# Pool products of a hybrid decoder layer: three float32r passes from split operands, two attention units later, in place of native fp32

## The reference, cut to what matters

```python
h    = rms_norm(x, norm_mix_pre)
proj = h @ w_in                                   # (1024, 1792), split by columns
u_pool, g_b, g_c, u_conv, q, k, v = split(proj)   # 256, 256, 256, 256, 512, 128, 128
# pool mixer: per group g of 64 channels a causal trailing mean over 2, 4, 8, 16
# tokens, minus the token; then a 64x64 map of the group, and a scale per channel
d = mean_w(u_pool) - u_pool
y_pool = einsum('bsgc,gcd->bsgd', d, pool_w) * pool_scale
mix = concat(y_pool, y_conv, y_attn) @ w_o
x   = x + rms_norm(mix, norm_mix_post)            # then a gated conv-MLP, untouched here
```

## Time and profile before

| | |
|---|---|
| median of three runs | 950.24 us (950.16 to 950.44) |
| span of the profiled execution | 948.2 us, so 2.0 us less than the median |
| TensorE matmul, busy | 938.9 us, 99% |
| TensorE weight load, busy | 777.9 us, 82% |
| VectorE, busy | 654.7 us, 69% |
| ScalarE, busy | 433.5 us, 46% |
| GpSimd, busy | 189.4 us, 20% |
| DMA | 151.16 MB, mean 159 GB/s |

### The profile page before, as it was taken

The page is one execution under the profiler, slowest core; times in us unless marked ns, Lnnn a source line. Parts: engine busy times, 40 slices in busy tenths (PEclk is TensorE's granted clock), DMA queues, the critical chain, the costliest instruction groups (busy, mean ns, idle before and its releaser), DMA issues.

```text
span 948.2 us, 11487 instructions
## 1 busy us (share of the span) xinstructions
PE 938.9 (99%) x4419; PEld 777.9 (82%) x4419; DVE 654.7 (69%) x710; ACT 433.5 (46%) x648; POOL 189.4 (20%) x182
## 2 busy tenths in 40 slices
PE   8999999999999999999999999999999999999997
PEld 7988887887888888888888888888888888888886
DVE  6645795766655899777877787778776653535668
ACT  5524444444433555445443444444444454335353
POOL 3301000000111424242223333443431100000021
PEclk9999999999999999999999999999999999999999
DMA  6999971005322236486343446554647775677455
GB/s 225 269 328 231 209 145 45 23 23 178 134 89 89 90 97 206 142 184 183 115 141 100 145 112 133 112 143 105 140 91 208 201 235 214 228 267 264 163 171 200
DMA packets 114248, 151.16 MB, mean 159 GB/s; under 512 B 6289, under 2 KB 66193, under 8 KB 114193
## 3 DMA queue, kind: packets, MB, share of 16 engines
q1 hardware_dynamic: 100737, 118.63, 38.5%
q0 software_dynamic: 13456, 31.79, 16.8%
HBM read 113.17 MB, written 60.29 MB: 183 GB/s over the span
## 4 chain that ended last, share of the span: by engine, by line
PE 97%; DVE 1%; DMA 0%; ACT 0%; POOL 0%; issue 0%; DVEq 0%; POOLq 0%; SPq 0%; ACTq 0%
PE ps L1616 30%; PE ps L1618 30%; PE ps L1617 30%; PE ps L1626 1%; PE ps L1751 1%; PE ps L1774 1%; PE ps L1752 1%; PE ps L1760 1%; PE ps L1778 1%; DMA xin<-in_x 0%; DVE hlo L1138 0%; PE ps L1789 0%; DVE ps L1155 0%; PE ps L1664 0%; DVE x2b L1427 0%
## 5 line engine op out<-in xcount | busy, mean ns | idle before, releaser
L1616 PE MATMUL ps<-hhi,whi 128*128 128x512 f32 (+1 forms) x240 | 91.1, 379 | 0.5 <-DVE hlo L1138 0.5
L1618 PE MATMUL ps<-hhi,wlo 128*128 128x512 f32 (+1 forms) x240 | 88.5, 369 | 0.0
L1617 PE MATMUL ps<-hlo,whi 128*128 128x512 f32 (+1 forms) x240 | 88.5, 369 | 0.0
L686 POOL TENSOR_TENSOR w_sums<-wraw 128x1024 f32<-128x1024 f32 x20 | 48.4, 2421 | 185.8 <-DVE w2lo L1373 63.0
L648 POOL TENSOR_SCALAR meansq<-sumsq 128x1 f32<-128x1 f32 x28 | 10.0, 357 | 373.4 <-ACT yg L1042 170.8
L1616 PEld LDWEIGHTS ps<-hhi,whi 128*128 128x128 f32 x240 | 45.3, 189 | 8.0 <-DVE hlo L1138 0.7
L1001 ACT ACTIVATE yg<-ps,par_b 128x1024 f32<-128x1024 f32 x21 | 25.3, 1207 | 57.9 <-DVE ps L1499 57.9
L1618 PEld LDWEIGHTS ps<-hhi,wlo 128*128 128x128 f32 x240 | 45.2, 189 | 7.7
L1617 PEld LDWEIGHTS ps<-hlo,whi 128*128 128x128 f32 x240 | 45.3, 189 | 7.4 <-issue 0.5
L1447 DVE SCALAR_TENSOR_TENSOR yg<-ps,par_a,yg 128x1023 f32<-128x1023 f32 x22 | 28.2, 1282 | 26.9 <-ACT yg L1001 26.9
L1616 PE MATMUL ps<-h2hi,whi 128*128 128x512 f32 x116 | 45.4, 391 | 0.2 <-DVE wraw L1148 0.2
(11 more groups left out here) (261 smaller groups left out, 2709.1 us busy)
## 6 DMA issues: line engine op xcount, KB each, us to landing
wraw<-in_ffn_w_up SPq DMA_DIRECT2D x42, 512.0 KB, 5.2
s_dram<-in_ffn_w_down POOLq DMA_DIRECT2D x6, 2816.0 KB, 28.1
wraw<-r_dram SPq DMA_DIRECT2D x44, 256.0 KB, 3.7
wraw<-s_dram SPq DMA_DIRECT2D x44, 256.0 KB, 4.9
r_dram<-cst SPq DMA_DIRECT2D x33, 256.0 KB, 2.8
wraw<-act_dram SPq DMA_DIRECT2D x33, 256.0 KB, 3.6
wraw<-in_ffn_w_down SPq DMA_DIRECT2D x33, 256.0 KB, 4.6
wraw<-in_w_in SPq DMA_DIRECT2D x14, 512.0 KB, 10.2
```

The source lines that it names most:

```text
L686: pool.tensor_tensor(w_sums[:, 0:2, :], raw[:, 0:4:3, :], raw[:, 2:3, :].broadcast_to([P, 2, HALF]), ALU.add)\
L1616: pe.matmul(acc, w_hi, x_hi, start=first, stop=False, skip_group_check=looped)
L1617: pe.matmul(acc, w_hi, x_lo, start=False, stop=False, skip_group_check=looped)
L1618: return pe.matmul(acc, w_lo, x_hi, start=False, stop=last, skip_group_check=looped)
```

## The change

The pool products go from slots 8 and 10 to slots 10 and 12. Each is made of three float32r passes in place of one native fp32 matmul, through the helper `product`. For that both operands are split. ScalarE rounds `pool_mat` after the exponentials of unit 6, the first half of `pool_d` after the evacuation in unit 8, and the second half in unit 10, behind the copy of the first product, into the same tile `pool_hi`. VectorE makes the low parts in `mixer_work`: that of the matrix (128x256) in unit 7 ahead of the longer sums, that of the first half (128x1024) in unit 9, and that of the second in unit 11 ahead of the conv taps. The copies of the products follow their slots, to units 10 and 12. The new tiles lie over space that is free at that time.

```diff
-POOL_SLOT = (8, 10)
+POOL_SLOT = (10, 12)
...
+            def round_pool_mat():
+                act.wait_ge(pool_w_in, 64)
+                act.activation(pool_mat_hi[:, :, :], pool_mat[:, :, :], ACT.Copy)\
+                   .then_inc(pool_mat_rounded, 1)
+
+            def round_pool(i):
+                if i == 0:
+                    act.wait_ge(pool_ready, 2)
+                else:
+                    act.wait_ge(pool_mixed, 1)
+                act.activation(pool_hi[:, :], pool_d[:, i, :], ACT.Copy).then_inc(pool_rounded, 1)
...
                 exps(u)
                 if u in POOL_SLOT:
                     copy_pooled(POOL_SLOT.index(u))
+                if u == 6:
+                    round_pool_mat()
                 if u == 8:
                     evacuate(2)
+                    round_pool(0)
+                if u == POOL_SLOT[0]:
+                    round_pool(1)
...
+            def low_pool_mat():
+                dve.wait_ge(pool_mat_rounded, 1)
+                dve.tensor_tensor(pool_mat_lo[:, :, :], pool_mat[:, :, :], pool_mat_hi[:, :, :],
+                                  ALU.subtract).then_inc(pool_mat_split, 1)
+
+            def low_pool(i):
+                dve.wait_ge(pool_rounded, i + 1)
+                dve.tensor_tensor(pool_lo[:, i, :], pool_d[:, i, :], pool_hi[:, :], ALU.subtract)\
+                   .then_inc(pool_split, 1)
...
             def mixer_work(u):
 
                 s = u // 2 - 2
+                if u == 7:
+                    low_pool_mat()
                 if u == 8:
                     pool_means(1)
+                if u == 9:
+                    low_pool(0)
+                if u == 11:
+                    low_pool(1)
...
             def pool_product(i):
-                if i == 0:
-                    pe.wait_ge(pool_w_in, 64)
-                pe.wait_ge(pool_ready, i + 1)
+                pe.wait_ge(pool_mat_split, 1)
+                pe.wait_ge(pool_split, i + 1)
                 pe.wait_ge(s_masked, POOL_SLOT[i] + 1)
                 for c in range(2):
-                    last = pe.matmul(ps[:, 4 + c, :], pool_mat[:, i, :],
-                                     pool_d[:, i, c * HALF:(c + 1) * HALF],
-                                     start=True, stop=True)
+                    cols = slice(c * HALF, (c + 1) * HALF)
+                    last = product(ps[:, 4 + c, :], pool_mat_hi[:, i, :], pool_mat_lo[:, i, :],
+                                   pool_hi[:, cols], pool_lo[:, i, cols], True, True)
                 last.then_inc(pool_mixed, 1)
```

More of the change, by code:

```diff
@@ L174, in build @@
         par_rows = alloc(xb_, "par_rows", [P, 2, P])
+        pool_mat_hi = alloc(xb_, "pool_mat_hi", [P, 2, P], F32R)
         xb_.close()
@@ L180, in build @@
         xb2.close()
+        xb3 = ExitStack()
+        alloc(xb3, "under_pool_hi", [P, 3 * SEQ])
+        pool_hi = alloc(xb3, "pool_hi", [P, SEQ], F32R)
+        alloc(xb3, "under_pool_lo", [P, 2 * SEQ + 3 * PAD])
+        pool_lo = alloc(xb3, "pool_lo", [P, 2, SEQ], F32R)
+        alloc(xb3, "under_pool_mat_lo", [P, NT, P])
+        pool_mat_lo = alloc(xb3, "pool_mat_lo", [P, 2, P], F32R)
+        xb3.close()
         xc = ExitStack()
@@ L319, in build @@
         pool_ready = sem("pool_d_ready")
+        pool_mat_rounded = sem("pool_weights_rounded")
+        pool_mat_split = sem("pool_weights_split")
+        pool_rounded = sem("pool_d_rounded")
+        pool_split = sem("pool_d_split")
         pool_mixed = sem("pool_product_done")
```

## The result

The changed kernel takes **953.44 us** (median of five, 952.30 to 954.87), the kernel before on the same chip 950.24 (950.16 to 950.59). The ratio is 1.0032, with a 95% interval of 1.0021 to 1.0042: slower, by more than the +1.96 us of the forecast, and outside its range by 0.24 us. The five times of the changed kernel fall into two groups, 952.30 and 952.36, and 953.44, 953.62 and 954.87. Those of the kernel before do not. Among so few executions the median can fall into either group. The profiled execution is one of the first group (952.30 us, span 950.5).

A forecast was written before the change was run, and what follows sets the result against it. TensorE was taken to bound the kernel: waits of 2.38 and 0.26 us less 0.68 saved in the products give +1.96, and 948.2 + 1.96 + 2.04 = 952.2 us. The range was 950.9 to 953.2.

The forecast's parts named there:

- What bounds the kernel: TensorE, at full clock, has no idle time after 21.14 us, so each us won or lost there counts.
- The products' saving: On TensorE, two pool products of six fp32r passes each, 1.37 us in place of 1.71: -0.68 us.
- The chain of the first wait: TensorE's turning of unit 9's probabilities waits for VectorE's normalisation: lead 1.71, less room 1.06, plus lateness 1.73; 2.38 us.
- ScalarE's 0.95: In unit 8, rounding pool_d's first half ahead of the copies delays the copy of unit 9's scores by 0.95 us.
- The second wait: TensorE waits 0.26 us before unit 12's product, for masking on VectorE delayed by low_pool(1) in unit 11.
- The sum of +1.96: Whole kernel: waits of 2.38 and 0.26 less the 0.68 saved in the products, +1.96 us.
- rival 3: TensorE's clock falls to 1.2 GHz through the wait, 1.2 to 3.5 us more: 953.4 to 955.7; chance 0.06.
- The sign: Whole kernel against a bound of about 0.2%, 1.9 us: slower 0.55, same 0.42, faster 0.03.
- Rival 1: At unit 9's turning, idle time covers the three additions; wait 0.65 against 0.68 saved: 950.2 us; chance 0.10.
- Rival 2: A heavier chain in units 11 and 12: the second wait grows to some 1.3 us, 953.3; chance 0.07.
- Rival 4: Passes on pool tiles run at the native rate, four per half, so no saving: +2.64, 952.9 us; chance 0.02.
- the sum of +2.2: Total if VectorE operations do not overlap, each added subtraction costing some 0.1 us more: about +2.2 us.

The follow-up runs named there:

- the run without the first wait: Changed kernel with the turning of unit 9's probabilities moved behind the first half of slot 10's projection on TensorE; 949.84 us.
- both waits gone: Changed kernel with unit 9's turning behind the first half of slot 10's projection and low_pool(1) at the end of unit 10; 949.66 us.
- the move alone: Kernel before with its two native fp32 products moved to slots 10 and 12, nothing else; 950.91 us.
- moving the rounding: Changed kernel with ScalarE's rounding of pool_d's first half behind the copy of unit 9's scores; 951.22 us.
- the wait alone: Kernel before with four unread VectorE operations, about 4.2 us, ahead of unit 9's normalisation; six executions 952.42 to 954.51 us, ratio 1.0034.
- the longer wait: Kernel before with about 5.7 us of unread VectorE work ahead of unit 9's normalisation; five executions 953.99 to 956.72 us, ratio 1.0053.
- the filled wait: Changed kernel with eight unread fp32r passes on TensorE before unit 9's turning, after waiting for the masking of unit 8; 952.19 us.

## Why the prediction was right or wrong

**Right, by its steps.** What bounds the kernel, and that nothing later absorbs a wait: the run without the first wait is 2.46 us below the lower group's median, as much as the wait cost (2.33) within the spread. The products' saving: 0.68 forecast, 0.64 read in the trace; the medians with both waits gone differ by 0.69, though their interval takes in no change. The chain of the first wait, lead 1.71 less room 1.06 plus lateness 1.73: its first two parts by the move alone (0.64 for 0.65), the whole by the profile (2.33 for 2.38), ScalarE's 0.95 by moving the rounding (951.22 for 951.2). The second wait: 0.21 for 0.26, and 0.18 between the medians without it (949.84 and 949.66). The sum of +1.96 holds for the lower group, whose seven executions have their median at 952.30. The profile of the lower group showed each thing that the prediction named as the mark of its forecast.

**Wrong: the clock.** The sum has no term for the clock behind the wait. The step that failed is the one that put it at nothing: rival 3, "The clock falls in the wait", with its chance of 0.06 and the argument against it, "the work before and behind the wait is dense". Dense work around the gap does not keep the clock up in every execution. With a gap of 2.1 us eight of fifteen executions are in the upper group, and in the two of them that were profiled the granted clock went to 0.50; the median of the first five therefore belongs to the case that I had priced at 953.4 to 955.7 and nearly left out of the range. Its price was of the right size: 1.2 to 3.5 us forecast, some 1.7 measured (1.6 in the passes of the execution of 954.21). That the first median fell just there was in part chance: three of five lay in the upper group, and the next eight had theirs at 952.43, inside the range. With an even chance for it the range would have reached past 954. The trace of before had no gap of that size, so it could not give the chance; what it could have given is that 0.06 was far too sure for something that no row showed. The rule cited there, the Trainium skill's (TensorE: Matmul & The Clock Gate, "What's actually happening"), that the engine is throttled unless its activity releases it, agrees with the traces of the upper group (clock 0.50 behind 2.12 us of idle time). By itself it does not tell what the two profiles of the lower group show: an idle time of the same length and a clock that stays at 1.00.

**The sign** stands: slower by over 0.2% was given 0.55, and it is slower by 0.32%. But it lies clear of the bound only through the clock: in the lower group alone it would have been 0.2%, at the bound, and the interval of the next eight executions (1.0015 to 1.0036) reaches below it.

**The other rivals.** Rival 1, that the additions are covered, did not happen, but its figure of 0.65 for the bare lead is what the move alone shows. Rival 2 did not happen: the second wait is small. Rival 4 did not: 1.39 us for six passes. VectorE's pitch stayed at 1.13 behind an operation of 1.22 (153.09 to 154.22), so the rows held, and the sum of +2.2, in which nothing overlaps, did not. The section of the Trainium skill that the prediction draws on there (VectorE: DVE Perf Modes, "The DRAIN you can't avoid") adds that a next operation that is not held starts earlier, which the prediction left out and these rows agree with.

**A wrong step afterwards.** In the expectation for low_pool(0) behind the normalisation I took off its whole pitch, though two paths meet there: VectorE's, 1.73 late, and ScalarE's exponentials, 1.29 late. Taking work off the first buys only the difference, 0.44.

## What to carry to other kernels

A saving in the stream of the engine that sets the end pays only if those who feed it keep up: moving work later lets that engine run ahead, and its lead turns into a wait where a chain on the other engines has less room than the lead (here 1.06 us of room for a lead of 1.71). Read the room there (old start less old release) before moving anything; and put added work on the feeding engines behind what the bound engine waits for, or move the waiting step behind work that is ready, which here turned +3.2 us into -0.5, and with both waits gone -0.7, neither told from no change. A gap on TensorE may cost more than its length, and may do so in some executions only: where a forecast has a gap of two us or more at full clock (2.1 did it here), give the clock a chance of its own, and read the times one by one, since a single profile can miss it.

## What the runs showed of the hardware that was not expected

| TensorE idle at one place | executions in an upper group, 1.7 us or more above the others |
|---|---|
| 0.42 us (the move alone) | 0 of 11 |
| 1.19 us (rounding behind) | 0 of 11 |
| 1.68 us (low_pool(0) behind) | 0 of 11 |
| 2.12 to 2.13 us (the changed kernel) | 8 of 15 |
| 2.17 us (the wait alone) | 3 of 6 |
| 3.67 us (the longer wait) | 3 of 5 |
| 2.4 us late, filled with passes | 0 of 11 |

In the three profiled executions of the upper groups the granted clock goes from 2.4 to 1.2 GHz at the end of the gap or behind it, and returns a few us later. With the longer wait it falls as the turning starts (158.6 us); in the two of the changed kernel dense work has begun again by then (it falls at 156.0 behind a turning at 155.2, and at 157.0, after the turning at 155.8 and three further passes). Whether it falls differs between executions of one program. Between 1.68 and 2.12 us of idle time these runs pass from never to about half; they do not show where between, nor whether it would be the same elsewhere in a kernel. The runs of the table lie on several chips: those with 0.42 and 2.17 us on one, those with 1.68 and 3.67 us and the filled wait on a second, the one with 1.19 us on a third. The changed kernel had its upper group on the first (3 of 8) and on the third (2 of 2), so a difference between chips does not explain the rows of those two; the changed kernel beside the filled wait and beside 1.68 us, on the second, is missing. One execution of the move alone lay 0.9 us above its median, and five of the kernel before (of the 67 that ran beside the experiments) 0.8 to 1.0 above theirs; nothing was profiled of these, and their cause is open.
